# New merge orders for the four engines in the mixer stage of a hybrid recurrent trunk

## The chip, the cores and the metric

The kernel is one program on one core of a Trainium2 chip. The metric is device time in microseconds (us) of one execution, as the median of three runs. The engines named below are PE (TensorE, the matrix engine), DVE (VectorE), ACT (ScalarE), POOL (GpSimd) and SP (SyncE, which here issues DMAs). Each has its own instruction queue and works through it in order; a semaphore wait on one instruction holds everything behind it on that engine.

## The reference

Two layers of a decoder trunk run on 320 tokens: 256 of one prompt and 8 new tokens of each of 8 sequences, model width 1024. Each layer does

```python
h = rmsnorm(x, W['norm_mix'][i])
cp = h @ W['w_in'][i]
ya, sh, Sa = rwkv7_mixer(ca, s_shift[i], s_rwkv[i], ...)    # RWKV-7 time mixing, 6 heads
yb, Sb = retention_mixer(cb, s_ret[i], pos0, ...)           # retention, 4 heads
yc, cv, hc = mamba2_mixer(cc, s_conv[i], s_ssm[i], ...)     # Mamba-2 SSD, 6 heads
x = x + jnp.concatenate([ya, yb, yc], axis=-1) @ W['w_out'][i]
h = rmsnorm(x, W['norm_ffn'][i])
x = x + swiglu(...)   # layer 0;   layer 1: top 2 of 8 experts, moe_swiglu(...)
```

and returns the outputs and every group's recurrent state, for the prompt and for the 8 sequences. All of it is in float32.

## The kernel before, in words

Activations stay on the chip, transposed (features on the partitions, 320 tokens along a row). Weights stream from HBM in slots of 128x1024 floats (SP's queue, a ring of 11). Each slot is split in two parts: ACT copies it to `whi` (line 1472), DVE subtracts to get `wlo` (line 1981), and PE makes each product in three passes (lines 619 to 621).

A layer has four stages: input norm and input projection with the mixers, output projection, feed-forward norm, feed-forward or experts. Only the second half of the first stage is touched here. In it the 28 remaining slots of the input projection run merged with the three mixers. Every mixer is cut into short pieces, and each engine has its own list of which piece comes next. In the lists:

- `in` is a piece of the input projection. On PE it is half a slot (12 products). On ACT the pieces of one slot are the split of a later slot (line 1472) and the copy of the result out of PSUM; on DVE they are the split of a later slot (line 1981) and, for the RWKV columns, the token shift (lines 2093 to 2095), which reads the PSUM bank and so frees it.
- `prep` is the RWKV preparation (decays, keys, bonus), `inv0` to `inv2` the triangular inversions of the three token blocks (prompt 0 to 127, prompt 128 to 255, samples), `cb`, `tok`, `rw` the RWKV chunk products, transposes and recurrence; `sS`, `nS`, `xs`, `xv` the RWKV sample states.
- `rot` and `rt0` to `rt2` are the retention, `conv`, `dt` and `mb0` to `mb2` the Mamba-2 group, `shift` an output DMA, `out` the start of the output projection (on ACT and DVE: the splits of its first two slots).

The helper `weave` walks a list and takes from the named part its code up to the next `yield`. The lists are the strings `PE_TURNS` (181 pieces), `ACT_TURNS` (136), `DVE_TURNS` (226) and `POOL_TURNS` (29), and the same lists serve both layers. Within a part the order is fixed; only how the parts interleave is chosen by the lists. The waits in the code of each piece are on constants and don't depend on the lists.

Some pieces matter later. `inv` on PE: line 785 forms the matrices and waits for DVE's last `prep` products (lines 2146, 2151); line 795 transposes what DVE wrote at line 2220; lines 802, 809, 813 are the levels of the inversion. `rw` on PE: line 881 multiplies the `Rs` that DVE copied (line 2262), ACT copies the result to `SA` (line 1663), line 613 (`mx`) accumulates; after the last chunk ACT copies the outputs to `kp` (line 1667), and lines 908, 912 and 918 are the group norm. `mb` on DVE: line 2427 scales the sample states. ACT's functions lie in table sets, and where the next function is of another set than the last, an ACT_TABLE_LOAD stands in front of it.

After the lists, PE multiplies the 8 slots of the output projection.

Of the kernel before, what the change touches and what calls it, by code (L numbers as in the profile page):

```python
# [143 lines left out]
for _n, _w in [("g_mix", 8), ("g_ffn", 8), ("g_fin", 8), ("mu", A_TILES), ("w0", 3), ("a0", 3), ("k_k", 3),  # L144
# [39 lines left out]
ACT_TURNS = """
    dt in in in in prep prep in in in in prep prep in in prep in in prep in in prep prep in in in in in in in in
    in in in in prep conv in in prep conv prep in in conv in in sS dt dt tok2 conv tok2 dt in in in in conv tok2
    in conv in conv in rw2 in in in in in rw2 rw2 in in mb0 mb0 tok0 in in tok0 mb0 in in rt0 in mb0 mb0 tok0 in
    mb1 rw0 mb1 in mb0 rw2 mb1 rt0 rt0 rw0 mb1 rw0 rw0 mb1 rw0 mb1 tok1 mb2 tok1 tok1 mb2 rt0 rw0 mb2 rw1 rt0
    mb2 rt1 rt1 rt1 rw1 rt1 mb2 mb2 rt1 out out rw1 rw1 rw1 rt2 rw1 rt2 rt2 rt2 rt2
"""  # L190
DVE_TURNS = """
    prep in in in in in in in prep in in in in in in prep in in in prep in prep prep in prep prep in inv2 inv1 in
    inv0 inv1 in inv1 inv0 inv2 inv0 inv2 in inv2 in prep inv0 inv1 inv2 in inv2 inv0 inv1 conv conv conv conv inv1
    in conv conv inv0 inv2 conv conv inv1 inv0 inv2 in conv inv0 conv conv conv cb2 cb2 inv1 inv0 inv0 inv0 in inv1
    conv conv dt conv conv inv0 dt inv1 dt dt dt dt dt dt inv0 inv1 dt dt dt inv0 dt dt in conv conv conv conv in
    conv conv conv conv in conv conv inv1 conv conv rw2 in xs inv1 inv1 in xs nS nS rot xs nS cb0 nS rw2 in nS nS
    rw2 in cb0 cb0 mb0 in rot rot mb0 rt0 rt0 in in in in rw2 mb0 rw2 mb0 rw2 mb0 mb0 mb0 mb0 mb0 mb0 rw0 mb1 rw0
    mb0 rw2 mb1 rw0 mb1 mb1 mb1 mb1 mb1 mb1 rw0 cb1 cb1 cb1 mb1 mb1 rw0 mb1 mb2 rw0 rt0 rw0 rw0 rt0 rw0 rw1 mb2 rt0
    rt0 mb2 mb2 rt0 rw1 rt1 rt1 mb2 mb2 mb2 rw1 rt1 rt1 mb2 mb2 rt1 rt1 rw1 mb2 rt1 out out rt2 rt2 rw1 rw1 rw1 rw1
    rw1 rt2 rt2 rt2 rt2 rt2 rt2  # L200
"""
# [2873 lines left out]
```

## Time and profile before

| | us |
|---|---|
| median of 3 runs (1288.71 to 1290.39) | 1289.28 |
| the profiled execution's own time | 1288.66 |
| its span | 1286.8 |
| PE busy | 1229.0 (96%) |
| DVE busy | 920.9 (72%) |
| ACT busy | 716.3 (56%) |
| POOL busy | 131.5 (10%) |
| merged stage of layer 0 | about 25 to 262 |
| merged stage of layer 1 | about 542 to 781 |

All stretches are in us from the start of the span. The two merged stages are 476 of the 1286.8 us. "PE busy" includes time in which a product runs at half the clock, so the granted clock has to be read beside it.

### The profile page before, as it was taken

The numbers are of one execution on the slowest core, as the hardware profiler recorded it, in microseconds if no ns is written. First come the engines' busy times: TensorE is split into PE (matmuls) and PEld (weight loads), VectorE is DVE, ScalarE is ACT, GpSimd is POOL, SyncE is SP. The second block draws the span as 40 slices with busy tenths as digits, with TensorE's granted clock in tenths as the row PEclk, the third lists the DMA queues.
The fourth block names the chain that finished last, engine by engine and source line by source line (L and its number), as shares of the span: only waits on it lengthen the run. The fifth ranks groups of instructions, "written<-read, shape, count | busy, mean of one in ns | idle before, by whom it ended". The sixth has DMA issues, their size and how long they took to land.

```text
span 1286.8 us, 27073 instructions
## 1 busy us (share of the span) xinstructions
PE 1229.0 (96%) x10557; PEld 1098.7 (85%) x10557; DVE 920.9 (72%) x1477; ACT 716.3 (56%) x1109; POOL 131.5 (10%) x161
## 2 busy tenths in 40 slices
PE   7989999899999999998999989899999999999996
PEld 6979888789999999997988878887888788788785
DVE  7576755666555557857675565588989989998996
ACT  6633345234433334472434534577877878777784
POOL 1021310210000000102121012001010110101010
PEclk9999999789999999999999988999999999999998
DMA  8321331155445443242133106389979979997992
GB/s 295 120 85 46 111 106 35 73 198 188 150 152 168 152 147 132 75 134 70 54 119 107 35 23 232 122 292 330 341 256 356 323 263 344 324 354 253 358 323 104
DMA packets 63835, 236.35 MB, mean 184 GB/s; under 512 B 7536, under 2 KB 7760, under 8 KB 63088
## 3 DMA queue, kind: packets, MB, share of 16 engines
q1 hardware_dynamic: 60960, 221.51, 49.1%
q0 software_dynamic: 2336, 12.81, 2.7%
q8 instruction: 77, 1.26, 0.4%
q10 hardware_dynamic: 432, 0.52, 0.1%
q14 instruction: 30, 0.25, 0.1%
HBM read 225.41 MB, written 8.09 MB: 181 GB/s over the span
## 4 chain that ended last, share of the span: by engine, by line
PE 82%; DVE 10%; ACT 4%; issue 4%; DMA 0%; DVEq 0%; ACTq 0%
PE bank L619 12%; PE bank L621 11%; PE bank L620 11%; PE bank L1409 8%; PE bank L1386 6%; PE bank L1388 6%; PE bank L1387 6%; PE bank L613 3%; PE bank L1306 2%; DVE wlo L1981 2%; ACT whi L1472 2%; PE bank L813 1%; PE bank L802 1%; PE bank L809 1%; PE bank L1351 1%
## 5 line engine op out<-in xcount | busy, mean ns | idle before, releaser
L1472 ACT ACTIVATE whi<-wraw 128x1024 fp32r<-128x1024 f32 x407 | 428.8, 1059 | 354.7 <-PE bank L621 292.5
L1981 DVE TENSOR_TENSOR wlo<-wraw,whi 128x1024 fp32r<-128x1024 f32 x407 | 501.4, 1245 | 170.4 <-ACT whi L1472 162.9
L619 PE MATMUL bank<-hh,whi 128*128 128x320 f32 x576 | 189.1, 328 | 12.6 <-DVE Dx L2095 6.4
L621 PE MATMUL bank<-hh,wlo 128*128 128x320 f32 x576 | 180.5, 313 | 0.0
L620 PE MATMUL bank<-hl,whi 128*128 128x320 f32 x576 | 180.5, 313 | 0.0
L1386 PE MATMUL bank<-whi,hh 128*128 128x512 f32 (+1 forms) x384 | 147.4, 384 | 3.4 <-DVE wlo L1981 2.9
L1388 PE MATMUL bank<-wlo,hh 128*128 128x512 f32 (+1 forms) x384 | 143.5, 374 | 0.0
L1387 PE MATMUL bank<-whi,hl 128*128 128x512 f32 (+1 forms) x384 | 143.3, 373 | 0.0
L619 PEld LDWEIGHTS bank<-hh,whi 128*128 128x128 f32 x576 | 110.3, 191 | 23.9 <-issue 7.9
L619 PE MATMUL bank<-rawh,whi 128*128 128x320 f32 x384 | 119.8, 312 | 0.5 <-DVE rawl L2538 0.3
L621 PE MATMUL bank<-rawh,wlo 128*128 128x320 f32 x384 | 118.9, 310 | 0.0
L620 PE MATMUL bank<-rawl,whi 128*128 128x320 f32 x384 | 118.9, 310 | 0.0
L620 PEld LDWEIGHTS bank<-hl,whi 128*128 128x128 f32 x576 | 110.7, 192 | 0.0
L621 PEld LDWEIGHTS bank<-hh,wlo 128*128 128x128 f32 x576 | 110.5, 192 | 0.0
L1386 PEld LDWEIGHTS bank<-whi,hh 128*128 128x128 f32 x384 | 72.2, 188 | 22.0 <-DVE wlo L1981 6.5
L1388 PEld LDWEIGHTS bank<-wlo,hh 128*128 128x128 f32 x384 | 72.3, 188 | 13.3
L1387 PEld LDWEIGHTS bank<-whi,hl 128*128 128x128 f32 x384 | 72.4, 189 | 10.2
L619 PEld LDWEIGHTS bank<-rawh,whi 128*128 128x128 f32 x384 | 72.6, 189 | 1.1 <-DVE rawl L2538 0.6
L620 PEld LDWEIGHTS bank<-rawl,whi 128*128 128x128 f32 x384 | 72.6, 189 | 0.1
L621 PEld LDWEIGHTS bank<-rawh,wlo 128*128 128x128 f32 x384 | 72.5, 189 | 0.0
L2939 POOL TENSOR_TENSOR x<-x,yt 128x320 f32<-128x320 f32 x28 | 27.2, 992 | 393.3 <-ACT yt L1884 392.9
L619 PE MATMUL bank<-hidh,whi 128*128 128x320 f32 x184 | 56.9, 309 | 1.6 <-DVE hidl L2538 1.0
(427 smaller groups left out, 2084.4 us busy)
## 6 DMA issues: line engine op xcount, KB each, us to landing
wraw<-in_w SPq DMA_DIRECT2D x410, 512.0 KB, 5.0
smb<-in_s_ssm POOLq DMA_DIRECT2D x2, 1536.0 KB, 8.0
out_o_ssm<-smb POOLq DMA_DIRECT2D x2, 1536.0 KB, 7.2
cst<-in_consts SPq DMA_DIRECT2D x1, 2097.0 KB, 13.3
srw<-in_s_rwkv POOLq DMA_DIRECT2D x2, 768.0 KB, 5.9
out_o_rwkv<-srw POOLq DMA_DIRECT2D x2, 768.0 KB, 3.7
x<-in_x SPq DMA_DIRECT2D x2, 640.0 KB, 4.9
cBs<-cB SPq DMA_DIRECT2D x16, 80.0 KB, 2.1
```

Of the source, the lines that this page charges most:

```text
L613: return pe.matmul(out, lhsT, rhs, start=start, stop=stop, skip_group_check=True)
L619: mm(out, hi, rh, start=first, stop=False)
L620: mm(out, hi, rl, start=False, stop=False)
L621: return mm(out, lo, rh, start=False, stop=last)
L1306: m = mm(B[bk][:, (k % 2) * 2 * P:(k % 2 + 1) * 2 * P], htk[z][:, q, k * P:(k + 1) * P], pick[:, q, :, :], start=(q == 0), stop=(q == 2))
L1386: mm(out, hh[:, k, ours], whi[:, r % HI, cols], start=(k == 0), stop=False)
L1387: mm(out, hl[:, k, ours], whi[:, r % HI, cols], start=False, stop=False)
L1388: m = mm(out, hh[:, k, ours], wlo[:, POS[r], cols], start=False, stop=(k == KT - 1))
L1409: m = mm(B[4 + z][:, :], h_[:, f, 0:P], w_[:, z * 512:(z + 1) * 512], start=(f == 0 and q == 0), stop=(f == FT - 1 and q == 2))
L1472: af(whi[:, ring % HI, :], wraw[:, POS[ring], :], ACT.Copy).then_inc(S("slot_hi"), 1)
L1981: tt(wlo[:, POS[ring], :], wraw[:, POS[ring], :], whi[:, ring % HI, :].bitcast(F32), ALU.subtract).then_inc(S("slot_split"), 1)
L2939: tt(x[:, m_, :], x[:, m_, :], yt[:, m_ // 2, :], ALU.add).then_inc(S("yt_free"), 1)
```

## The change

Only the four lists change. Each part's pieces are the same in number and in inner order. On DVE three `in` pieces that hold no instruction come last in the list instead of in the middle. No tile, no buffer, no wait and no operation of the program is edited. Two lines of PE's list stand for the kind of edit:

```diff
-    in in in in in in in in prep in in in in in in in prep in in in prep in in in in in inv2 inv1 inv0 in inv1 inv2
-    inv0 in inv2 in prep inv2 inv0 inv1 in in inv1 inv0 inv2 prep inv1 in inv0 inv2 in inv1 inv0 cb2 cb2 sS sS sS
+    in in in in in in in in prep in in in in in in in prep in in in prep in in in in in in inv2 inv1 inv0 in in inv2
+    inv1 inv0 prep inv2 inv1 in in inv2 inv0 inv2 inv1 inv0 inv1 inv0 prep in in inv0 inv1 in sS inv0 inv2 sS inv0
```

What it does to the instructions at three places, in layer 0 (layer 1 has the same lists):

DVE, end of the RWKV preparation, before. Lines 2144, 2146 and 2151 are the last preparation products, 1981 is a weight split, 2093 to 2095 the token shift of a projection result:

```order
L2144 TENSOR_TENSOR aa<-X_84,aa 128x960
L1981 TENSOR_TENSOR wlo<-wraw,whi 128x1024
L2146 TENSOR_TENSOR aa<-aa,Pi 128x960
L2151 TENSOR_TENSOR Pi<-kp,Pi 128x960
L2093 SCALAR_TENSOR_TENSOR Dx<-bank,par,Dx 128x255
L2094 SCALAR_TENSOR_TENSOR Dx<-bank,par,Dx 128x8x7
L2095 SCALAR_TENSOR_TENSOR Dx<-sh_in,par,Dx 128x8
L2217 TENSOR_TENSOR A<-bank,cst 128x192
```

DVE, the same place, now:

```order
L2144 TENSOR_TENSOR aa<-X_84,aa 128x960
L1981 TENSOR_TENSOR wlo<-wraw,whi 128x1024
L2093 SCALAR_TENSOR_TENSOR Dx<-bank,par,Dx 128x255
L2094 SCALAR_TENSOR_TENSOR Dx<-bank,par,Dx 128x8x7
L2095 SCALAR_TENSOR_TENSOR Dx<-sh_in,par,Dx 128x8
L2146 TENSOR_TENSOR aa<-aa,Pi 128x960
L2151 TENSOR_TENSOR Pi<-kp,Pi 128x960
L1981 TENSOR_TENSOR wlo<-wraw,whi 128x1024
L2217 TENSOR_TENSOR A<-bank,cst 128x192
```

The token shift now stands ahead of the last two preparation products. On PE the matching change is one more half slot ahead of the first inversion product, and two half slots instead of one between the first and the second.

ACT, end of the merged stage, before. Here `s_rr` and `ysq` are norms of the retention and of Mamba, `SA` and `kp` belong to the last RWKV block, `hh` is an operand of the output projection, and the two `whi` rows are the splits of the first two slots of the output projection:

```order
L1663 ACTIVATE SA<-bank 128x192 [waits rw_SA]
L1699 ACTIVATE s_rr<-bank,cst 128x4 [waits rt_ms]
L1730 ACTIVATE ysq<-bank,cst 128x64 [waits mb_ms]
L1734 ACTIVATE hh<-cZ 128x3x64 [waits slot_used,mb_y3]
L1704 ACTIVATE hh<-cB 128x2x128 [waits slot_used,rt_y]
L1472 ACTIVATE whi<-wraw 128x1024 [waits slot_used,slot_in0]
L1472 ACTIVATE whi<-wraw 128x1024 [waits slot_used,slot_in1]
L1667 ACTIVATE kp<-bank 128x3x128 [waits rw_y]
L1670 ACTIVATE Pi<-bank 128x3x128 [waits rw_yd]
```

ACT, the same place, now:

```order
L1699 ACT_TABLE_LOAD
L1699 ACTIVATE s_rr<-bank,cst 128x4 [waits rt_ms]
L1730 ACTIVATE ysq<-bank,cst 128x64 [waits mb_ms]
L1663 ACTIVATE SA<-bank 128x192 [waits rw_SA]
L1667 ACTIVATE kp<-bank 128x3x128 [waits rw_y]
L1734 ACTIVATE hh<-cZ 128x3x64 [waits slot_used,mb_y3]
L1670 ACTIVATE Pi<-bank 128x3x128 [waits rw_yd]
```

One `whi` split went about 20 rows ahead, the other behind the retention's last norm; `kp` follows `SA` directly, and `SA` itself stands behind two norms.

ACT, middle of the merged stage, now. `xs` is the convolution's activation, `stage` a copy of a projection result, `d_wk` an exponential of the Mamba decays:

```order
L1646 ACTIVATE tok<-bank 128x192 [waits rw_tr]
L1472 ACTIVATE whi<-wraw 128x1024 [waits slot_used,slot_in10]
L1568 ACT_TABLE_LOAD
L1568 ACTIVATE xs<-cvx 128x256 [waits cv_done]
L1569 ACTIVATE xs<-cvx 128x64
L1558 ACTIVATE stage<-cv_in 128x8x3 [waits cv_kept,cv_done,slot_used]
L1559 ACTIVATE stage<-bank 128x8x8
L1560 ACTIVATE stage<-bank 128x256
L1634 ACT_TABLE_LOAD
L1634 ACTIVATE d_wk<-bank 128x18 [waits dt_cum]
L1663 ACTIVATE SA<-bank 128x192 [waits rw_SA]
L1568 ACT_TABLE_LOAD
```

The third convolution's activation stood ahead of the sample-state copies and all exponentials of the decays before; now it comes after a weight split that needs a later slot. In one layer's lists there are 22 table loads in all, and there were 19.

## Rows read from the trace of the kernel before

**Rows 1.** The page: busy us, share of the span, instructions.

```profile
PE 1229.0 (96%) x10557; PEld 1098.7 (85%) x10557; DVE 920.9 (72%) x1477; ACT 716.3 (56%) x1109; POOL 131.5 (10%) x161
```

**Rows 2.** Busy time by stretch: length, PE, PEld, DVE, ACT, POOL, clock, DMA.

```profile
25.00:262.00 237.00, 223.16 (x3044) 200.07 (x3042) 151.69 (x332) 108.16 (x216) 43.78 (x47) 0.96 0.26 86
262.00:540.00 278.00, 276.00 (x1873) 273.61 (x1874) 170.92 (x246) 112.44 (x157) 3.72 (x6) 0.99 0.46 152
542.00:781.00 239.00, 225.26 (x3046) 202.02 (x3045) 152.27 (x334) 108.45 (x217) 44.81 (x53) 0.95 0.26 86
```

**Rows 3.** Waits of PE, 25 to 255: who, for whom, sum, times, longest.

```profile
PE bank L619 <- DVE Dx L2095: 3.2, 2, 3.1
PE bank L881 <- DVE Rs L2262: 2.2, 2, 1.5
PE bank L619 <- ACT cZ L1548: 1.4, 1, 1.4
PE bank L908 <- ACT kp L1667: 1.3, 1, 1.3
PE bank L813 <- DVE Wm L2230: 1.1, 1, 1.1
PE bank L795 <- DVE Wm L2220: 1.0, 1, 1.0
...
PE bank L837 <- DVE srw_p L2271: 0.6, 1, 0.6
```

**Rows 4.** Timeline of DVE, end of preparation: start, us, what.

```profile
66.45 1.60 DVE L1981 TENSOR_TENSOR wlo<-wraw,whi 128x1024 fp32r<-128x1024 f32 x1
67.97 1.27 DVE L2146 TENSOR_TENSOR aa<-aa,Pi 128x960 f32<-128x960 f32 x1
69.27 1.52 DVE L2151 TENSOR_TENSOR Pi<-kp,Pi 128x960 f32<-128x960 f32 x1
70.72 0.47 DVE L2093 SCALAR_TENSOR_TENSOR Dx<-bank,par,Dx 128x255 f32<-128x255 f32 x1
71.29 0.34 DVE L2095 SCALAR_TENSOR_TENSOR Dx<-sh_in,par,Dx 128x8 f32<-128x8 f32 x1
```

**Rows 5.** Timeline of PE, four waits, idle time before in brackets.

```profile
71.69 0.41 PE L619 MATMUL bank<-hh,whi 128*128 128x320 f32 x1 [3.06 <-DVE Dx L2095]
...
176.86 0.41 PE L619 MATMUL bank<-hh,whi 128*128 128x320 f32 x1 [1.42 <-ACT cZ L1548]
...
237.66 0.91 PE L881 MATMUL bank<-Rs,TT 64*64 64x64 f32 x12 [1.50 <-DVE Rs L2262]
...
246.29 0.91 PE L908 MATMUL bank<-kp,cst 128*128 128x384 f32 x2 [1.29 <-ACT kp L1667]
```

**Rows 6.** Timeline of DVE: a split in the middle, state scaling near the end.

```profile
145.09 3.70 DVE L1981 TENSOR_TENSOR wlo<-wraw,whi 128x1024 fp32r<-128x1024 f32 x1 [1.72 <-ACT whi L1472]
...
233.53 3.69 DVE L2427 TENSOR_TENSOR smb<-smb,ecb 128x512 f32<-128x512 f32 x6
```

**Rows 7.** Timeline of ACT near the end of the stage.

```profile
222.36 1.28 ACT L1699 ACT_TABLE_LOAD   x1
223.66 0.26 ACT L1699 ACTIVATE s_rr<-bank,cst 128x4 f32<-128x4 f32 x1
...
243.88 1.99 ACT L1472 ACTIVATE whi<-wraw 128x1024 fp32r<-128x1024 f32 x2
245.77 0.47 ACT L1667 ACTIVATE kp<-bank 128x384 f32<-128x384 f32 x1
```

**Rows 8.** Stretches around the clock's falls, columns as in rows 2.

```profile
200.00:237.60 37.60, 33.14 (x690) 28.97 (x688) 25.62 (x70) 16.51 (x34) 1.14 (x2) 1.00 0.06 17
237.60:244.50 6.90, 6.84 (x80) 6.27 (x82) 3.68 (x15) 2.22 (x6) 1.66 (x3) 0.51 0.15 52
247.90:264.90 17.00, 16.74 (x142) 14.01 (x143) 8.31 (x20) 3.69 (x9) 9.31 (x8) 0.50 0.44 156
587.00:592.00 5.00, 3.20 (x14) 2.87 (x14) 1.74 (x4) 0.37 (x2) 1.98 (x3) 0.72 0.24 94
```

More of the change, by code:

```diff
@@ L175 @@
 PE_TURNS = """
-    in in in in in in in in prep in in in in in in in prep in in in prep in in in in in inv2 inv1 inv0 in inv1 inv2
-    inv0 in inv2 in prep inv2 inv0 inv1 in in inv1 inv0 inv2 prep inv1 in inv0 inv2 in inv1 inv0 cb2 cb2 sS sS sS
-    inv0 in inv0 in inv0 inv1 sS inv0 dt tok2 inv1 inv0 tok2 inv1 in inv0 dt in in in tok2 in in inv1 rw2 in in rw2
-    inv1 in in inv1 nS in cb0 nS rw2 in nS rw2 in rw2 in mb0 cb0 cb0 in tok0 in tok0 mb0 in in rt0 rw2 mb0 rt0 in in
-    mb0 in mb0 tok0 in rw0 mb1 rw0 in in rw0 rw0 mb1 rw0 mb1 rt0 rw0 mb1 rw0 rw0 cb1 rw0 mb1 cb1 cb1 rw0 tok1 mb2
@@ L181 @@
-    tok1 tok1 rw0 rt0 rt0 rw1 mb2 rt0 rw1 mb2 rw1 rw1 rt1 mb2 rt1 rw1 rt1 rt1 rw1 rt1 mb2 rt1 rw1 rw1 rw1 rt2 rw1
-    rt2 rw1 rt2 out out rt2 out rt2 rt2
+    in in in in in in in in prep in in in in in in in prep in in in prep in in in in in in inv2 inv1 inv0 in in inv2
+    inv1 inv0 prep inv2 inv1 in in inv2 inv0 inv2 inv1 inv0 inv1 inv0 prep in in inv0 inv1 in sS inv0 inv2 sS inv0
+    sS inv0 in cb2 sS cb2 inv1 dt tok2 inv0 inv1 tok2 inv0 tok2 in in in in dt rw2 inv1 in rw2 inv1 inv0 in in in in
@@ L183 @@
+    in inv1 nS rw2 cb0 in in nS inv1 rw2 in rw2 nS cb0 in mb0 cb0 in in tok0 tok0 rw2 mb0 in mb0 in rt0 tok0 in rt0
+    in mb0 in mb0 in rw0 mb1 in in rw0 mb1 rw0 rw0 mb1 rw0 rt0 rw0 mb1 rw0 rw0 cb1 cb1 rw0 rt0 mb1 cb1 rt0 rw0 tok1
+    tok1 mb2 tok1 rw0 mb2 rw1 mb2 rt0 rw1 rw1 rt1 mb2 rw1 rt1 rw1 rt1 mb2 rt1 rt1 rw1 rt1 rw1 rw1 rw1 rt2 out rw1
+    rt2 rw1 rt2 out rt2 out rt2 rt2
 """
 ACT_TURNS = """
-    dt in in in in prep prep in in in in prep prep in in prep in in prep in in prep prep in in in in in in in in
@@ L186 @@
[L186 to L189, printed above, removed]
+    in in in in prep in in prep in prep prep in in in prep in in prep in in in prep prep in in in in in in in in dt
@@ L190 @@
+    in in in in in prep in prep conv in in in conv sS dt dt tok2 tok2 in in prep tok2 in conv in dt rw2 conv conv in
+    in in in in in in conv in rw2 in rw2 in mb0 conv in in tok0 mb0 mb0 in in in tok0 mb0 mb0 rt0 tok0 in mb1 mb1
+    rw0 rw2 mb1 in mb0 rw0 rt0 mb1 rt0 rw0 rw0 mb1 rw0 out tok1 rt0 mb1 tok1 mb2 tok1 mb2 mb2 rw1 rw0 rt0 rt1 mb2
+    rt1 rt1 rt1 mb2 rw1 rw1 mb2 rw1 rt1 rw1 rt2 rt2 rw1 rt2 rt2 out rt2
 """
 DVE_TURNS = """
-    prep in in in in in in in prep in in in in in in prep in in in prep in prep prep in prep prep in inv2 inv1 in
@@ L193 @@
[L193 to L197, printed above, removed]
@@ L198 @@
-    mb0 rw2 mb1 rw0 mb1 mb1 mb1 mb1 mb1 mb1 rw0 cb1 cb1 cb1 mb1 mb1 rw0 mb1 mb2 rw0 rt0 rw0 rw0 rt0 rw0 rw1 mb2 rt0
-    rt0 mb2 mb2 rt0 rw1 rt1 rt1 mb2 mb2 mb2 rw1 rt1 rt1 mb2 mb2 rt1 rt1 rw1 mb2 rt1 out out rt2 rt2 rw1 rw1 rw1 rw1
-    rw1 rt2 rt2 rt2 rt2 rt2 rt2
+    prep in in in in in in in in prep in in in in in prep in in in prep in prep prep in in prep prep in inv2 in inv2
+    inv1 inv0 inv2 inv0 prep inv1 in inv0 in inv1 inv0 inv2 inv1 inv1 inv2 conv conv conv in inv2 inv0 conv conv
+    inv1 conv inv0 conv inv2 inv0 conv inv1 in conv inv0 conv conv inv0 in inv1 inv2 inv0 inv0 cb2 conv cb2 conv
@@ new lines @@
+    inv1 conv dt conv inv0 in dt inv1 dt conv dt dt dt dt dt inv0 dt dt dt conv dt conv inv1 rw2 conv conv conv dt
+    conv in in in conv conv conv conv inv0 inv1 xs conv conv inv1 in nS rw2 in nS xs in inv1 xs nS cb0 rot nS nS nS
+    cb0 rw2 mb0 cb0 in rot rot mb0 rt0 mb0 rt0 rw2 rw2 mb0 in mb0 mb0 mb0 mb0 mb0 mb0 in rw2 rw0 mb1 mb1 rw0 mb1 mb1
+    rw0 mb1 mb1 mb1 rw0 mb0 cb1 mb1 rw2 cb1 cb1 mb1 mb1 rw0 mb1 mb2 rw0 rt0 rw0 rt0 rw1 rw0 mb2 mb2 rt0 mb2 rt0 rw1
+    rt1 rt1 mb2 mb2 mb2 rw1 rt1 rt0 rt1 mb2 mb2 rt1 out rw1 rt1 mb2 rw0 rt2 rt2 rw1 rw1 rw1 rw1 rt2 rw1 rt2 rt1 rt2
@@ L201 @@
+    rt2 rt2 out rt2 in in in
 """
 POOL_TURNS = """
-    prep prep shift conv conv prep conv conv conv conv xv conv conv rot xv xv xv xv mb0 rot mb1 mb2 rt1 conv mb1 rt2
-    mb2 mb2 rt2
+    prep prep conv conv conv prep xv conv conv conv xv conv xv rot conv xv rot mb0 xv mb1 mb2 rt2 mb2 shift rt2 rt1
+    conv mb2 mb1
 """
```

## The prediction

> **What bounds the kernel now.** I read the page first, then the busy time by stage, then PE's own waits, and last the timelines around each wait. The page [rows 1] shows PE busy 96% of the span, so only PE's idle time and its time at a low clock can be won by an order. The stretches [rows 2] say where that is: from 262 to 540 PE is busy 276.0 of 278 us, while each merged stage has it idle 13.8 us (237.0 − 223.16; 239.0 − 225.26 = 13.7 in layer 1). DVE is busy 64% and ACT 46% there, so neither is a bound by its sum; what ends PE's waits is one late instruction at a time. The list of PE's waits [rows 3] names them: the six largest and one of 0.6, 10.8 us together; the first is a projection product (L619) that once stands 3.1 us for the token shift L2095. Layer 1 runs the same lists and has the same idle time, so everything below is worked for one layer and doubled.
>
> The clock is the second loss. Near the end of the stage the granted clock is 0.5, which is 1.2 GHz instead of 2.4, for 6.9 and 17.0 us [rows 8], after 37.6 us in which PE was busy 33.14, or 88%.
>
> **The change part by part.** The operations stay, so no busy time of PE, DVE or POOL goes or comes. ACT gets 3 table loads more a layer at 1.28 us each [rows 7], 3.8 us on an engine with 129 us idle in the stage (237.0 − 108.16 [rows 2]). What counts is which wait ends when.
>
> Place A, 66 to 90 us. Before, DVE finishes a split at 68.05, then does the two products L2146 and L2151, and only then the token shift, which ends at 71.63 [rows 4]; PE, waiting since 68.63 (71.69 − 3.06 [rows 5]), goes on at 71.69. Now the shift comes directly after the split. It takes 0.92 us from its first start to its last end, so it ends at 68.97 and PE goes on at about 69.0, 2.7 us earlier. The products it overtook end 0.9 us later, at about 71.7. PE has two half slots before it needs them instead of one; a half slot is 12 products at 0.147 us each (276.0 us for 1873 of them [rows 2]), 1.8 us, so PE comes to the inversions at 72.5 and doesn't wait. At that point it has done 1.8 us more work than before and stands 1.0 us earlier (before: 71.69 + 1.8 = 73.5), together 2.8. Next, the wait of L795 for L2220 (1.0 us) has two half slots over it instead of one and should go; following DVE's new row of work I find two new short waits, 0.1 us at the second inversion group and 0.5 at the third, because the bonus products L2155 now stand ahead of one L2220. Place A: −2.8 − 1.0 + 0.6 = −3.2 us.
>
> Place B, 100 to 150. The wait of L813 for L2230 (1.1 us [rows 3]) came after a split that took 3.70 us [rows 6], where the one in rows 4 took 1.60; while it ran, POOL was in the rotary products of the retention. That POOL piece now stands behind two RWKV state pieces, and no split of DVE starts while it runs. −1.1. Against that, ACT's third convolution activation now waits behind a weight split for a later slot and pays a load of 1.28; DVE's next convolution tap waits for it, and the `Rs` copy and a split stand behind the tap. I follow this to two new waits of PE, 0.5 and 0.8 us: +1.3. The bounds are 0, if the split is ready one slot earlier than I think, and +3.7, if a whole load and a whole activation piece come on top twice over. I take 1.3, as the rows nearest to it (1.0 to 1.4 [rows 3]) are waits of this kind.
>
> Place C, 176.9. L619 waits 1.42 us for ACT's L1548, a table load and a copy behind a split [rows 5]. PE now has about 1.5 us more of other work (a transpose group and a norm product) in front of it. −1.4.
>
> Place D, 205 to 262. Four waits change. L837 (0.6 [rows 3]) goes because DVE updates the RWKV state ahead of the Mamba state. The 1.50 us before L881 at 237.66 comes from the six scalings that hold DVE 3.69 us [rows 6]; they still stand in front, but PE now has two more norm sums and the second half of a chunk to do meanwhile. −1.5. The 1.29 us before L908 goes: ACT did two splits, 1.99 us, just ahead of `kp` [rows 7], and now does none there. −1.3. A new table load stands in front of `s_rr`, 1.28, with some 0.5 us of it uncovered; DVE's `cZ` chain comes 0.6 us later since the sum in front of it waits its turn, and PE's cover for that is a transpose group. Together +0.9. The later `mb` pieces come up to 1 us earlier, which gives the retention's last block the same. −1.0. Place D: −0.6 − 1.5 − 1.3 + 0.9 − 1.0 = −3.5. The bounds are −6.5, all waits shown for this place plus the second half-clock piece shortened, and +1.
>
> Here a rule of the Trainium skill bears on the added loads. The rows have the load at 1.28 us and the function 0.02 us behind its end [rows 7]. The page "ScalarE: Activation LUTs", section "What ACT_TABLE_LOAD costs", adds a drain of about 1.38 us to the 1.28 of every switch, 2.66 in all; by it the three new loads would cost ACT 8.0 us a layer instead of 3.8 and the new waits in places B and D would be some 2.8 us longer, two loads of 1.38 more, which makes 1278 of the forecast (my estimate from that page). The trace shows no such drain, so the sum keeps 1.28.
>
> Past the lists nothing should come late. The second `whi` and `wlo` split for the output projection now stand near the end, but PE first has the rest of one slot, 2.2 us, to do. POOL issues four output DMAs ahead of its last state product, about 2.3 us; PE wants that product 12 us later. If this cover were gone it would cost those 2.3 us a layer.
>
> Sum for a layer: −3.2 − 1.1 + 1.3 − 1.4 − 3.5 = −7.9 us; for two, −15.8. The profiled execution took 1288.66 us (span 1286.8, and 1.9 around it), 0.6 under the median. 1288.66 − 15.8 = 1272.9, so I say 1273.
>
> **The rivals.**
>
> 1. *Given back in the middle.* From 90 to 165 us PE would run about 3 us ahead of its old times, but DVE and ACT have to keep up, with more inversion pieces in a row on PE and fewer projection products over them. The old order had almost no wait from 100 to 145. For it: three of my covers there are under 0.5 us. Against: DVE is only 64% busy. If place A and B come to nothing (−3.2 − 1.1 + 1.3 = −3.0), −4.9 a layer remains, and if half of D goes too, −3.2. Time: about 1281.
>
> 2. *The clock stays up.* If the waits that go in place D keep PE above the share it had before the fall, the 17.0 us at 0.5 [rows 8] shorten. At most 8.5 us of it could go; the hand-overs between ACT, DVE and PE in the last retention block (ACT and DVE pieces of 0.3 to 0.6 us between PE pieces) take back about half. −4.5 a layer more: 1264. For it: PE was only 12% idle ahead of the fall. Against: waits of 0.6 remain in the same stretch, and the pieces there stay small.
>
> 3. *Slower, by the clock in the middle.* Should the new waits in place B be 2 us each and follow closely, PE would be as idle as in layer 1 at 587 to 592, 3.20 of 5 us busy and a clock of 0.72 [rows 8]. Around 120 to 140 us PE does projection products back to back, so a stretch like the one of 17.0 us at half would cost its whole 8.5 us. With 4 − 1.3 = 2.7 us more waiting, −7.9 + 2.7 + 8.5 = +3.3 a layer, 1295. It decides from a stretch of about 10 us at half on (7.9 − 2.7 = 5.2 us lost). For it: the order of ACT there is the one thing that looks worse than before. Against: in layer 0 the 3.1 us wait of place A made no fall.
>
> 4. *The orders change, and nothing comes of it.* The waits move to other instructions and sum to the same 13.8 us, as PE's chains are as long as before. 1288.7. For it: every piece has the same inputs. Against: places A and the `kp` row are plain, a wait that stands behind work that it doesn't need.
>
> **How the numbers follow.** The forecast has a chance of 0.47, rival 1 0.20, rival 2 0.13, rival 3 0.10, rival 4 0.10. The predicted time is 1273. The range of 8 in 10 runs from 1261, under rival 2 with its fullest clock gain, to 1287, over rival 1. No change means within 0.2%, 2.6 us, about what a measurement of this kernel can tell. Faster: 0.47 + 0.20 + 0.13, and a little of rival 4: 0.81. Same: 0.08. Slower: 0.11.
>
> **What would show it.** In the profile after: PE's wait at L619 for L2095 under 0.5 us, and the sum of PE's waits in the merged stage of layer 0 near 6 (13.8 idle before, less 7.9); L813 for L2230, L619 for L1548, L837 for L2271 and L908 for `kp` gone from PE's waits; new waits at L881 or L619 around 125 to 140 us of about 1.3 together; the merged stage ending near 254 instead of 262; two falls of the clock at its end still there. I am wrong if PE's idle time in the stage stays above 11 us a layer, if the granted clock falls in the middle of a merged stage, or if it stays up at the end.

## The result

The changed kernel took 1274.08 us (median of 4 runs, 1271.64 to 1275.14), the kernel before 1289.84 in the same comparison (4 runs, 1288.71 to 1292.28): a ratio of 0.9873, 95% interval 0.9852 to 0.9893. It is faster by 1.3%, and 1273 was forecast. The sections below show that the time came out almost as forecast by luck: two steps of the forecast failed, with errors of opposite sign. Of the 56 executions of the kernel before that were recorded with their clock, one had a mean clock of 0.737 and a span of 1507.3 us; it is left out everywhere.

The page of the profiled execution after (1275.14 us, span 1273.3), the row that answers to [rows 1]:

```profile
PE 1217.8 (96%) x10557; PEld 1092.2 (86%) x10557; DVE 920.4 (72%) x1477; ACT 721.5 (57%) x1115; POOL 132.2 (10%) x161
```

The span is 13.5 us shorter, and PE's busy time, with the same 10557 products, is 11.2 us shorter. So PE's idle time fell by only 2.3 us in the whole kernel, where the forecast wanted 15.8. A busy time that shrinks at an unchanged count of products points at the clock: mean clocks of 0.974 and 0.980 over the two spans are 66.9 and 50.9 us at half clock. The busy time by stretch, columns as in [rows 2]:

```profile
25.00:262.00 237.00, 224.51 (x3074) 203.89 (x3073) 153.62 (x338) 112.10 (x220) 43.79 (x47) 0.96 0.26 88
262.00:540.00 278.00, 275.36 (x1875) 272.36 (x1874) 173.86 (x250) 114.74 (x161) 7.39 (x16) 1.00 0.45 153
542.00:781.00 239.00, 226.53 (x3092) 205.52 (x3091) 154.15 (x335) 114.31 (x222) 45.05 (x49) 0.96 0.28 91
```

From 25 to 262 us PE is idle 12.5 us (13.8 before), although this stretch now holds 6.6 us of the next stage. PE's waits in layer 0, as in [rows 3]:

```profile
PE bank L619 <- DVE Dx L2095: 2.2, 3, 1.2
PE bank L619 <- ACT cZ L1548: 1.5, 1, 1.5
PE bank L1035 <- ACT rsq L1696: 1.2, 1, 1.2
PE bank L1078 <- DVE seg L2378: 1.2, 1, 1.2
PE bank L802 <- DVE TT L2238: 0.9, 1, 0.9
PE bank L809 <- DVE Wm L2230: 0.9, 1, 0.9
PE bank L619 <- DVE wlo L1981: 0.9, 1, 0.9
PE bank L619 <- ACT cB L1544: 0.8, 1, 0.8
...
PE bank L908 <- ACT kp L1667: 0.6, 1, 0.6
...
PE bank L881 <- DVE Rs L2262: 0.5, 1, 0.5
```

The list is longer and its rows are smaller. L813, L795 and L837 are gone as forecast, and L908 is halved. Both old waits of L881 (at 225 and 238 us) are gone; the 0.5 shown is a new one at 138. L619 for `cZ` stayed, and most of the others are new.

To say where time went, both traces need points of equal work. PE's list has 181 pieces (one name of the list each), and at its 49th and 138th piece both orders have done exactly the same pieces. The 49th comes at about 100 us, in the triangular inversions; the 138th is a read product (L837) of RWKV block 1, at about 212. Up to the 49th, to the 138th and to the end of the stage, before:

```profile
25.00:101.20 76.20, 71.43 (x760) 66.19 (x760) 51.90 (x102) 39.89 (x82) 13.82 (x13) 1.00 0.32 108
101.20:211.94 110.74, 107.35 (x1602) 96.38 (x1600) 68.94 (x146) 48.50 (x93) 18.75 (x24) 1.00 0.27 86
211.94:261.12 49.18, 43.50 (x690) 37.38 (x689) 30.56 (x83) 18.89 (x40) 11.21 (x11) 0.80 0.14 52
```

and after:

```profile
25.00:98.70 73.70, 71.41 (x772) 67.18 (x771) 51.92 (x103) 37.92 (x75) 12.21 (x11) 1.00 0.34 113
98.70:213.00 114.30, 108.17 (x1590) 98.74 (x1591) 65.99 (x143) 53.91 (x103) 20.54 (x24) 0.97 0.25 83
213.00:255.40 42.40, 38.34 (x691) 32.13 (x690) 31.21 (x84) 17.95 (x39) 8.24 (x8) 0.90 0.14 52
```

Length less PE's busy time is idle time, and the third number from the right is the mean granted clock. A stretch at half clock is charged here with half its length. The head (first row) is 2.5 us shorter, all of it idle time. The middle is 3.6 us longer: idle time +2.7, 6.9 us at half clock where there was none, +3.4, and 2.6 less for the rest of the work. The tail is 6.8 us shorter: idle time −1.6 (5.7 to 4.1), and the clock 0.80 to 0.90, which is 19.7 us at half clock (2 x 0.20 x 49.18) against 8.5, −5.6. Layer 1 repeats it: its middle is 3.6 longer, its tail 6.7 shorter. Up to the tail the new order has gained nothing. Charged like this, most of what the tail gains is the clock; the runs e9 and the table below show that a microsecond at half clock costs nearer 0.3 than 0.5, which leaves the clock about half of it.

### The profile page after: what moved, and what is told of

Same layout as the page of the kernel before. It is cut to its first block, busy times and chain, and to the rows that moved or that the text cites. A ratio compares the mean times of both kernels' runs of the same rounds, so it can differ in the third digit from the quotient of the medians.

```text
span 1273.3 us, 27099 instructions
## 1 busy us (share of the span) xinstructions
PE 1217.8 (96%) x10557; PEld 1092.2 (86%) x10557; DVE 920.4 (72%) x1477; ACT 721.5 (57%) x1115; POOL 132.2 (10%) x161
## 3 DMA queue, kind: packets, MB, share of 16 engines
q1 hardware_dynamic: 60960, 221.51, 49.3%
q8 instruction: 77, 1.26, 0.4%
## 4 chain that ended last, share of the span: by engine, by line
PE 81%; DVE 8%; ACT 7%; issue 3%; DMA 0%; ACTq 0%; DVEq 0%
PE bank L619 12%; PE bank L621 11%; PE bank L620 11%; PE bank L1409 8%; PE bank L1386 6%; PE bank L1388 6%; PE bank L1387 6%; PE bank L613 4%; DVE wlo L1981 2%; PE bank L1306 2%; ACT whi L1472 2%; PE bank L802 1%; PE bank L1351 1%; PE bank L1335 1%; PE bank L813 1%
## 5 line engine op out<-in xcount | busy, mean ns | idle before, releaser
L619 PE MATMUL bank<-hh,whi 128*128 128x320 f32 x576 | 188.7, 328 | 13.5 <-DVE Dx L2095 4.5
L619 PEld LDWEIGHTS bank<-hh,whi 128*128 128x128 f32 x576 | 111.0, 193 | 22.7 <-issue 7.8
L619 PE MATMUL bank<-rawh,whi 128*128 128x320 f32 x384 | 120.2, 313 | 0.5 <-DVE rawl L2538 0.3
L1387 PEld LDWEIGHTS bank<-whi,hl 128*128 128x128 f32 x384 | 72.4, 189 | 10.2
L619 PEld LDWEIGHTS bank<-rawh,whi 128*128 128x128 f32 x384 | 73.0, 190 | 1.1 <-DVE rawl L2538 0.6
L1409 PE MATMUL bank<-whi,hidh 128*128 128x512 f32 x176 | 57.9, 410 | 0.6 <-DVE wlo L1981 0.6
```

The source lines that it names most:

```text
L619: mm(out, hi, rh, start=first, stop=False)
L1387: mm(out, hl[:, k, ours], whi[:, r % HI, cols], start=False, stop=False)
L1409: m = mm(B[4 + z][:, :], h_[:, f, 0:P], w_[:, z * 512:(z + 1) * 512], start=(f == 0 and q == 0), stop=(f == FT - 1 and q == 2))
```

## The experiments

Each kernel has the operations of the kernel before; where only lists differ, a hybrid follows one order up to a point of equal work and the other behind it, on all four engines. Each was timed in five rounds beside the kernel before.

**Run e1, the new head and middle.**

```diff
 PE_TURNS, pieces 26 to 49 (50 to 138 and the other engines' lists likewise)
-in inv2 inv1 inv0 in inv1 inv2 inv0 in inv2 in prep inv2 inv0 inv1 in in inv1 inv0 inv2 prep inv1 in inv0
+in in inv2 inv1 inv0 in in inv2 inv1 inv0 prep inv2 inv1 in in inv2 inv0 inv2 inv1 inv0 inv1 inv0 prep in
```

> New orders on all four engines up to PE's 138th piece (the first head norm of the Mamba chunks, about 212 us), the old orders behind it. Theory T (all of the gain lies behind that piece, since at it the new kernel stands 1.07 us later than the old in layer 0 and 1.1 us more behind than it began in layer 1): 1288.7 + 2 x 1.1 = about 1291, PE's idle time before 212 us about 8.4 us, the merged stage ending about 263. Rival F (the forecast's places A, B and C are worth -3.2 + 0.2 - 1.4 = -4.4 a layer): 1280. Rival I (the halves only work together): 1289 here and in the run of the other half.

(The 138th piece is not a head norm but the read product L837.) Measured: ratio 0.9989 (0.9973 to 1.0005), 1290.24 us. Theory T holds: the places A, B and C together, costed at −4.4 us a layer, brought nothing. In its trace the head is 2.6 us shorter and the middle 5.0 us longer than before, with 10.2 us at half clock in it.

**Run e2, the new tail.**

```diff
 PE_TURNS, pieces 139 to 162, and 163 to 181
-rw0 mb1 cb1 cb1 rw0 tok1 mb2 tok1 tok1 rw0 rt0 rt0 rw1 mb2 rt0 rw1 mb2 rw1 rw1 rt1 mb2 rt1 rw1 rt1
+cb1 rw0 rt0 mb1 cb1 rt0 rw0 tok1 tok1 mb2 tok1 rw0 mb2 rw1 mb2 rt0 rw1 rw1 rt1 mb2 rw1 rt1 rw1 rt1
-rt1 rw1 rt1 mb2 rt1 rw1 rw1 rw1 rt2 rw1 rt2 rw1 rt2 out out rt2 out rt2 rt2
+mb2 rt1 rt1 rw1 rt1 rw1 rw1 rw1 rt2 out rw1 rt2 rw1 rt2 out rt2 out rt2 rt2
```

> The complement: old orders up to PE's 138th piece, new orders behind it. T: -6.7 us a layer, the merged stage of layer 0 ending near 255, one fall of the clock of 3.4 us and one of 10.2 in it instead of 6.9 and 17.0; 1288.7 - 13.5 = 1275. F: place D alone, -3.5 a layer, 1281.7. I: 1289.

Measured: 0.9881 (0.9857 to 0.9905), 1277.64 us, nearly all of the change's gain. Theory T is nearest (2.6 us off); F is 4 us off and I falls. Its tails of layer 0 and 1:

```profile
213.30:255.90 42.60, 38.28 (x691) 32.63 (x690) 29.47 (x79) 17.93 (x39) 7.25 (x7) 0.92 0.14 50
725.20:769.10 43.90, 39.58 (x689) 33.41 (x688) 30.61 (x82) 17.93 (x39) 7.69 (x7) 0.87 0.15 49
```

**Runs e3 and e11, the head alone, and one step of it.** e3 takes the new orders up to the 49th piece (the diff of e1). e11 moves one piece of DVE's list:

```diff
 DVE_TURNS, end of the preparation
-in prep in prep prep in prep prep in inv2 inv1 in
+in prep in prep prep in in prep prep inv2 inv1 in
```

> New orders only up to PE's 49th piece (about 101 us), old ones behind it. In the two traces the new kernel is 2.5 us ahead at that piece in both layers. T (the lead is real and was lost behind it, to two waits of 0.9 us at 105 to 110 us and 6.8 us at half clock): the old middle waits only 0.15 us from 100 to 145, so the lead stays: 1288.7 - 5 = 1283.7. F: -3.2 a layer, 1282.3. Rival G (DVE and ACT are as late as before whatever PE does, so that any lead is given back by 118 us): 1288.7, with 2 us or more of new waits from 100 to 125.

> The kernel before with one step of DVE moved, and nothing on the other engines: the token shift (L2093 to L2095) ahead of the preparation's products L2146 and L2151. Forecast's place A without its half slots on PE: the wait of 3.06 us at 71.69 falls to 0.4; then the inversion comes 0.9 us later on DVE over one half slot of PE instead of two, at most 0.9 us of new wait: -1.8 to -2.7 a layer, 1285.1 to 1283.3. Rival Q (the swap alone is worth nothing, because the inversion that stood behind the products is then what PE waits for; the 2.85 us of the run e3 came from PE's half slots): 1288 to 1290, with a new wait of 2 us or more at L772 to L802 between 72 and 80 us.

Measured: e3 0.9942 (0.9919 to 0.9965), 1283.98 us, as theory T says, and rival G falls; e11 0.9931 (0.9913 to 0.9949), 1282.92, slightly more gain than its range. The waits of PE in e11 from 25 to 100 us:

```profile
PE bank L795 <- DVE Wm L2220: 1.0, 1, 1.0
PE bank L619 <- DVE Dx L2095: 0.3, 1, 0.3
PE bank L785 <- DVE Pi L2151: 0.2, 1, 0.2
```

The wait of 3.06 us [rows 5] is 0.33, the inversion's cover is short by 0.2 only, and PE stands 2.56 us earlier at the 49th piece, as against 2.66 in e3. So the token shift ahead of two products is nearly the whole of place A; rival Q falls. PE's shifted half slots and the removed wait of L795 are paid back by a new wait at 62.55 us, and the wait for the shift itself is still 0.88. DVE near 70 us, and PE's two waits, in the changed kernel:

```profile
68.24 1.60 DVE L1981 TENSOR_TENSOR wlo<-wraw,whi 128x1024 fp32r<-128x1024 f32 x1
...
70.33 0.34 DVE L2095 SCALAR_TENSOR_TENSOR Dx<-sh_in,par,Dx 128x8 f32<-128x8 f32 x1
70.60 1.15 DVE L2146 TENSOR_TENSOR aa<-aa,Pi 128x960 f32<-128x960 f32 x1
```

```profile
62.55 0.42 PE L619 MATMUL bank<-hh,whi 128*128 128x320 f32 x1 [1.21 <-DVE Dx L2095]
70.73 0.41 PE L619 MATMUL bank<-hh,whi 128*128 128x320 f32 x1 [0.88 <-DVE Dx L2095]
```

The long wait took the clock with it as well. Four traces have DVE's old order here (before, e2, e5, e9), and PE waits 3.1 us for L2095 in each of their eight heads. In seven of these 3.4 to 6.8 us at half clock follow at once; the fall at 589 [rows 8] is one of them. In the ten traces with the shift moved ahead no head of the twenty has a fall, and e11 differs from the kernel before in that one step only. The heads of layer 0 and layer 1, e2 and then e11 (those of layer 1 don't begin at the same piece, so that only their clock compares):

```profile
25.00:102.56 77.56, 72.89 (x760) 67.66 (x760) 51.86 (x102) 39.84 (x82) 13.81 (x13) 0.98 0.33 107
538.27:614.39 76.12, 71.82 (x753) 66.68 (x754) 50.25 (x101) 38.24 (x80) 13.80 (x13) 0.98 0.32 108
```

```profile
25.00:98.64 73.64, 71.86 (x763) 66.71 (x763) 51.30 (x102) 39.73 (x82) 13.91 (x13) 1.00 0.34 113
538.01:613.62 75.61, 73.22 (x769) 67.49 (x769) 53.27 (x106) 41.67 (x85) 16.65 (x23) 1.00 0.33 111
```

**Run e4, head and tail without the middle.** (The diffs of e1 for the pieces 26 to 49 and of e2, with the old pieces 50 to 138.)

> New orders up to PE's 49th piece, old ones from there to the 138th, new ones behind it: the two parts in which the new kernel gains, without the middle in which it loses. T with parts that add: 1275 - 5 = 1270. G: 1275, as with the tail alone. I: 1274 or more, not under the changed kernel.

Measured: 0.9793 (0.9766 to 0.9820), 1266.62 us. That is under the changed kernel, so I and G fall, and it is more than the gains of e2 and e3 together (23.5 us against 12.4 and 6.1); theory T's 1270 is 3.4 too high. Its old middle takes what the old middle took before, with a clock of 1.00:

```profile
98.66:209.20 110.54, 107.14 (x1591) 96.16 (x1592) 68.41 (x145) 50.09 (x98) 20.84 (x25) 1.00 0.27 87
```

What the new middle does wrong is in the changed kernel's timeline, all engines:

```profile
102.59 1.28 ACT L1568 ACT_TABLE_LOAD   x1
...
104.98 0.46 DVE L2108 TENSOR_SCALAR cvx<-stage,par 128x344 f32<-128x344 f32 x1 [7.18 <-ACT stage L1560]
...
105.47 0.35 DVE L2238 TENSOR_TENSOR TM<-TM,bank 128x192 f32<-128x192 f32 x1
...
106.24 0.92 PE L802 MATMUL bank<-TM,A 64*64 64x64 f32 x24 [0.93 <-DVE TT L2238]
...
109.30 0.89 PE L809 MATMUL bank<-Wm,TT 64*64 64x32 f32 x24 [0.91 <-DVE Wm L2230]
```

DVE stands idle for 7.18 us at a convolution tap that needs ACT's copy `stage`. ACT had itself waited 9.16 us for PE, until 100.53, to get a buffer for a split; then it does the split, a copy, the table load and an activation, and only then `stage`. In e4, which stands within 0.02 us of this kernel at the 49th piece, the load ran at 98.06, ahead of the split, and the tap began at 103.99, 1.0 us earlier. Behind the tap stands L2238, for which PE waits. The granted clock then falls:

```profile
110.28:117.10 6.82, 6.82 (x88) 6.70 (x85) 1.97 (x7) 0.00 (x0) 0.00 (x0) 0.51 0.01 2
```

This is half clock, 1.2 GHz, for 6.8 us, in both layers at the same place, the 3.4 us of the account above. All six new middles on record (the changed kernel, e1, e7) have such a stretch, of 6.8 to 10.2 us, and none of the sixteen old ones has.

**Run e6, less of the old middle.** (New again from the 87th piece.)

> New orders up to PE's 49th piece, old from there to the 86th (about 144 us), new ones behind it. Theory M (the new middle loses only from the 49th to the 86th piece, where its two waits of 0.9 us and 6.8 us at half clock are; from the 86th to the 138th the new kernel is 1.84 us faster than the old in both layers): 1266.6 - 3.7 = 1263. Rival N (those 1.84 us are only PE catching up on engines that had waited for it): 1266 to 1268.

Measured: 0.9807 (0.9778 to 0.9835), 1265.89 us, the same as e4. The middle took 110.07 us against 110.54; rival N holds, theory M falls. So what the new middle loses lies between the 49th and the 86th piece.

**Runs e9 and e10, the tail cut at the 162nd piece.** (The second pair of lines in the diff of e2: alone in e9; e10 is e6 with the first pair old again.)

> Old orders up to PE's 162nd piece (about 234 us), new ones for the last 19 of each layer. In the traces these 19 take 27.3 us in the old order (233.81 to 261.12) and 19.1 in the new (236.34 to 255.41), while the pieces from the 138th to the 162nd take 1.5 us more in the new. Theory L (the last 19 pieces hold all of the gain, by their own order): 1288.7 - 2 x 8.2 = 1272, under the run e2. Rival K (they are only quick because the new pieces ahead of them had fed ACT and DVE earlier, 1.5 us well spent): 1278 or more, above the run e2.

> The kernel of the run e6 with the old orders also from PE's 138th to its 162nd piece: new up to the 49th, old to the 86th, new to the 138th, old to the 162nd, new for the last 19. Theory L: 1.5 us a layer less than e6, 1265.9 - 3 = 1263. Rival K: 1266 to 1272, slower than e6.

Measured: e9 0.9909 (0.9886 to 0.9932), 1280.65 us; e10 0.9861 (0.9836 to 0.9885), 1273.35. Both are slower than theory L said and go rival K's way, e10 by 1.4 us more than it allowed: the pieces 139 to 162 belong to the gain. The trace of e9 shows more than it was made for. Its tails of layer 0 and layer 1, the same instructions in the same order:

```profile
214.33:264.06 49.73, 47.22 (x691) 40.37 (x690) 31.19 (x82) 18.49 (x39) 7.70 (x7) 0.70 0.12 44
733.93:776.30 42.37, 37.66 (x691) 31.98 (x690) 30.61 (x81) 18.42 (x39) 7.71 (x7) 0.93 0.15 52
```

Layer 0 has less idle time (2.5 against 4.7 us) and is 7.4 us longer, at a clock of 0.70 instead of 0.93. In one execution, at an equal order, the clock made a difference as large as the whole gain of a tail. It also gives a price: 29.8 us at half clock against 5.9, so 23.9 us more of it cost 7.4, or 0.31 us each, and not 0.5, since PE's waits shrink while its products take longer.

**Run e5, PE kept busy in the old tail.**

```diff
+            def keep_busy(out, n):
+                for _ in range(n):
+                    mm(out[:, 0:P], C("cmat"), C("ident"), start=True, stop=True)
...
+                    if (b, c) == (1, 1):
+                        keep_busy(B[3], 6)
                     pe.wait_ge(S("rw_Rc"), cb + c + 1)
...
+                if b == 1:
+                    keep_busy(B[2], 5)
                 pe.wait_ge(S("rw_yc"), it)
```

> The kernel before with its old orders, and products added that nobody reads: six products of 128 columns on PE just ahead of its wait for the second chunk of the last RWKV block (L881, 1.50 us of waiting at 237.66) and five ahead of its wait for kp (L908, 1.29 us at 246.29), about 0.22 us each by L997's rows, 1.3 and 1.1 us. Every other wait and every order is the old one. Theory C (the clock falls because PE stood idle, and most of the tail's gain is the clock): the 19.7 us at half clock per layer behind PE's 138th piece shrink to 10 or less, so 5 us or more a layer come back: 1279 or below, although no wait for another engine has gone. Rival W (the gain is the waits alone, and the clock falls through the narrow products that run there, 64 columns wide): 1289 to 1291, half-clock time unchanged.

Measured: 0.9983 (0.9954 to 1.0012), 1288.43 us. The median is rival W's, less 0.6 us. The profiled execution had 12.4 us at half clock in layer 0's tail and 20.0 in layer 1's. The filling worked at one of the two waits only: the 1.50 us ahead of L881 is gone, but the wait for `kp` is now 1.60 us behind the added products, and in layer 0 one of 2.12 for `rsq` comes later, with which the clock falls (line numbers behind the added lines are up by 9):

```profile
245.06 1.38 PE L853 MATMUL bank<-cst 128*128 128x128 f32 x10
248.04 0.91 PE L917 MATMUL bank<-kp,cst 128*128 128x384 f32 x2 [1.60 <-ACT kp L1676]
...
257.60 0.59 PE L1044 MATMUL bank<-cst,rsq 128*64 128x4 f32 x4 [2.12 <-ACT rsq L1705]
```

The 12 runs fall into two groups: six of 1283.5 to 1286.5 us with a mean clock of 0.983 or 0.984, a clock that no run of the kernel before had, and six of 1290.4 to 1296.9 us with 0.968 to 0.975. The mean clock is 0.978 against 0.972 for the kernel before in that comparison. So the added products do bring clock back, in half of the executions, and their own 3.0 us of PE's time a layer use it up: at an equal clock e5 is 2.5 us longer than the kernel before (table below). Theory C is supported by this, not shown: the waits were only in part filled, and no trace is from the faster group.

**Run e7, ACT's splits ahead of `kp` again.**

```diff
 ACT_TURNS
-mb1 rw0 out tok1 ... mb2 rw1 rw1 mb2 rw1 ... rt2 rt2 out rt2
+mb1 rw0 tok1 ... mb2 rw1 out out rw1 mb2 rw1 ... rt2 rt2 rt2
```

> The changed kernel with one thing undone: ACT's two weight splits for the output projection stand directly ahead of kp again. Forecast's term alone (the wait for kp is longer by 1.3 us a layer, the clock as it is): 1274 + 2.6 = 1276.7. Theory C (a longer wait there also makes the half-clock stretch that follows 3.4 us longer or more): 1274 + 2 x (1.3 + 1.7) = 1280. Rival W0 (PE's path at the end goes by the retention, and kp is covered): 1274.

Measured: 0.9869 (0.9839 to 0.9900), 1273.70 us, no change against the changed kernel. In its timeline ACT does both splits in a gap in which it had to wait for PE anyway (2.44 us in the changed kernel), and PE's wait is the 0.6 of the list above:

```profile
239.82 2.01 ACT L1472 ACTIVATE whi<-wraw 128x1024 fp32r<-128x1024 f32 x2
242.38 0.49 ACT L1667 ACTIVATE kp<-bank 128x384 f32<-128x384 f32 x1 [0.55 <-PE bank L613]
```

The forecast's reason for the term of `kp`, that it stood behind two splits [rows 7], is half of it. In the kernel before, the splits stood just behind two operand copies that wait for DVE:

```profile
243.55 0.42 ACT L1704 ACTIVATE hh<-cB 128x256 fp32r<-128x256 f32 x1 [0.61 <-DVE cB L2355]
```

So they began at 243.88 and ran past 245.00, when PE was done with what `kp` copies; `kp` began at 245.77, and that is the 0.7 us by which the wait shrank. The other 0.6 is the copy itself and is in every trace. In e7 the copies stand behind `kp`, and the splits are done in time.

**Runs e8 and e12, the last norm of the retention.** e8 changes PE's list of e4, e12 changes three lists of e6:

```diff
 PE_TURNS, the last five (e8 and e12)
-out rt2 out rt2 rt2
+out out rt2 rt2 rt2
 DVE_TURNS (e12)
-rw1 rw1 rw1 rw1 rt2 rw1 rt2
+rw1 rw1 rw1 rt2 rw1 rw1 rt2
 ACT_TURNS (e12)
-rt2 rt2 rw1 rt2 rt2 out rt2
+rt2 rt2 rt2 rw1 rt2 out rt2
```

> The kernel of the run e4 with one more step of order on PE: the third product group of the output projection ahead of the retention's last norm sum (L1035) instead of behind it, 1.06 us of work into a wait of 1.47 us. Theory: its operands are there (it never waited), so 1.06 us a layer go, 1264.5; by theory C the 6.8 us at half clock behind that wait shorten by 3.4 as well, 1.7 us more a layer: 1261. Rival: its operands come only after the norm sum, 1266.6 or slower.

> The kernel of the run e6 with three steps of order at the end of the merged stage: DVE adds the retention's last output (L2329, 0.27 us) ahead of the RWKV product L2293 (1.28 us) instead of behind it, ACT squares it (L1696) ahead of the RWKV copy L1679, and PE has the third product group of the output projection ahead of the norm sum L1035. In e6 that sum waits 1.5 us for the square. Theory D (the wait is made by what stands ahead on DVE and ACT, so that moving PE's group alone, in e8, only moved it): the wait goes, 0.4 to 0.6 us come back ahead of L1041, -1.0 us a layer: 1265.9 - 2 = 1264, with PE's idle time behind its 138th piece at 3.3 instead of 4.3 us. Rival E (the path at the end goes by the products and the sample states, which come no earlier): 1266, idle time 4 or more.

Measured: e8 0.9801 (0.9773 to 0.9828), 1265.78 us; e12 0.9782 (0.9764 to 0.9800), 1261.87, the fastest median here. In e8 the moved products ran ahead of L1035 without a wait, but its wait fell only from 1.47 to 1.03 us, and a new one of 0.55 stands ahead of L1041. So neither theory (1264.5) nor rival (1266.6 or slower) is confirmed; 0.8 us under e4, in another comparison, is no difference. The wait in e6, and the same place in e12:

```profile
246.24 0.40 PE L1035 MATMUL bank<-cst,rsq 128*64 128x4 f32 x4 [1.47 <-ACT rsq L1696]
```

```profile
248.31 0.40 PE L1035 MATMUL bank<-cst,rsq 128*64 128x4 f32 x4
...
249.97 0.45 PE L1041 MATMUL bank<-cst,s_rr 64*64 64x64 f32 x8 [1.26 <-DVE s_rr L2344]
```

The wait for the square is gone, as theory D has it, but the next one, for `s_rr`, took 1.26 us of it back: the path goes PE, ACT, DVE, PE, and PE has nothing left to put over it. Idle time in the tail is 4.2 us against 4.3, so theory D's 3.3 is wrong and rival E right on idle time. The median is 4.0 us lower than e6's all the same, with a mean clock of 0.989 against 0.986; e12 and e6 were not run side by side and their intervals overlap, so this last step isn't settled. That e4, e6, e8 and e12 beat both kernels is: their intervals lie below that of the changed kernel.

**All runs together.** Every run has a span and a mean granted clock, so orders and clock can be told apart without a profile. Within one kernel the span falls by 0.74 us for every 0.001 of clock (fitted within 14 kernels, 140 runs). As 0.001 of 1290 us is 2.6 us at half clock, this is 0.29 us for each of them, the price that e9's two tails gave. Taking every kernel's mean to a clock of 1 by that slope:

| kernel | runs | mean span | mean clock | span at clock 1 |
|---|---|---|---|---|
| before | 55 | 1289.3 | 0.972 | 1268.1 |
| after | 4 | 1271.9 | 0.982 | 1258.1 |
| e1 head and middle | 12 | 1288.7 | 0.969 | 1265.7 |
| e2 tail | 6 | 1275.4 | 0.982 | 1261.8 |
| e3 head | 7 | 1282.5 | 0.972 | 1261.5 |
| e4 head and tail | 5 | 1264.2 | 0.988 | 1255.0 |
| e5 filled waits | 12 | 1287.0 | 0.978 | 1270.6 |
| e6 less of the old middle | 6 | 1264.2 | 0.986 | 1254.0 |
| e11 one step | 6 | 1281.2 | 0.975 | 1262.6 |
| e12 norm first | 5 | 1261.2 | 0.989 | 1253.1 |

Of the 17.4 us between the means of before and after, 10.0 remain at equal clock and 7.4 are the clock's. For the tail alone (e2) it is 6.3 and 7.6 of 13.9; for the one step of the head (e11) 5.5 and 2.6 of 8.1. The middle takes clock away: e1 has the head's gain and yet the lowest clock of all. The traces agree on the tail. The eight old ones (before, e1, e3, e11) take 49.3 us on average with 19.7 at half clock, the ten new ones (after, e2, e4, e6, e7) 41.9 with 6.2; at 0.3 us each the clock is 4.1 of these 7.4, and the order 3.3.

## Why the number was right and the reasons half wrong

- **Place A, −3.2 a layer.** Right in mechanism, and a little large. −2.5 in the trace, −2.56 with the DVE step alone. Of the rest, L795's 1.0 us did go, but the new wait of 1.21 us at 62.55 was not seen, and the wait for the shift is 0.88 instead of under 0.5. What the step gives beside it, the half-clock stretch behind the old wait, up to 1.7 us in layer 1, was put at nothing, although its fall at 589 stood in [rows 8].
- **Place B, +0.2.** What was named came as named. L813's 1.1 us went, and where the third convolution's activation runs behind a split and a table load (133.86 to 135.14), two new waits stand, 0.46 and 0.89 us, forecast as 0.5 and 0.8:

```profile
137.89 0.56 PE L881 MATMUL bank<-Rs,TT 64*64 64x64 f32 x12 [0.46 <-DVE Rs L2262]
...
143.38 0.39 PE L619 MATMUL bank<-hh,whi 128*128 128x320 f32 x1 [0.89 <-DVE wlo L1981]
```

  The step that failed is what the forecast left out: the same mechanism at the first table load of this stretch, at 102.59, which put 0.93 and 0.91 us of waits at 105 to 110 and the half-clock stretch behind them. These were put at nothing. The runs e4 and e6 show that the loss lies there, between the 49th and the 86th piece; that it is this load and split which make it is read from the timeline, and no run moves them alone. The load itself was 1.28 us as in [rows 7] and the next function started 0.01 us later (102.59 + 1.28, then L1568 at 103.88), so the drain that the Trainium skill's page "ScalarE: Activation LUTs" ("What ACT_TABLE_LOAD costs") adds does not explain these waits.
- **Place C, −1.4.** Failed. The wait for `cZ` is 1.46 us, at 185, where it was 1.42. It is the length of one chain, from PE's last product on a buffer over ACT's split and load to the copy, and PE has 1.6 us of work beside that chain in either order, not 1.5 more. Two more waits came, 0.79 for `cB` at 171 and 0.64 at 176.
- **B and C together.** The middle costs +3.6 instead of saving 1.2, or +4.2 without L837's 0.6, which did go and was counted under place D.
- **Rival 3, a fall of the clock in the middle**, happened, on a smaller scale: 6.8 us at half, up to 3.4 lost, where it had 17 us and decided from 10. Because it was a rival and not a term, the sum lacked it.
- **Place D, −3.5.** The sign is right, the size half of it. The tail brought −6.8, beyond the bound of −6.5. By waits it was −1.6: both waits of L881 went and `kp` shrank, but by 0.7 and not 1.3 (e7), and the new waits for `seg` (1.2), `rsq` (1.2), `s_rr` (0.5) and `SA` (0.4) were costed at 0.9 together. The rest goes with the half-clock stretches, 19.7 us to 8.5, worth 3.4 to 5.6 us, which the forecast held fixed and gave only to rival 2, and there as "stays up". The two falls at the stage's end are still there as forecast, at 3.4 and 10.2 us instead of 6.9 and 17.0.
- **The sum.** −3.2, −1.2 and −3.5 were forecast, −2.5, +3.6 and −6.8 came in layer 0. The errors of +0.7, +4.8 and −3.3 leave −5.7 instead of −7.9. The other −7.8 are −3.4 up to layer 1's 49th piece, where the fall at 589 is gone, +3.6 and −6.7 in its middle and tail, and −1.3 behind them. A fall of 3.4 us at 821 is gone too, but that is chance: e5, e6, e8, e11 and e12 have one there. That all this adds up to −13.5 where −15.8 was forecast is luck. The conditions under which I had called myself wrong, over 11 us idle in the stage and a fall of the clock in its middle, are both met.

What stays open is what in the new tail keeps the clock up. Idle time isn't enough of an answer: e9's two tails contradict it, and e5's added products kept the clock up in half of its executions only. The Trainium skill's page "TensorE: Matmul & The Clock Gate", section "A second HAM failure mode: psum-queue depth-cycling", tells of a bf16 kernel with products of 512 columns in which frequent micro-idles between groups of products make the clock swing. The many short waits of these tails may be of that kind, yet no run here separates short waits from one long one.

## What to carry to other kernels

Compare two orders at points of equal work, and split each stretch into idle time, half-clock time and the rest, before you credit a wait; a busy time that falls at a constant count of products hints at the clock. Take the price of half-clock time from executions of one order, as waits shrink beside it. Cut a reordering at such points and run the parts: here one part of three lost what another won, and leaving it out gave −2.1% instead of −1.3%. Cost a table load or a split by what stands behind it on the next engine and on the one after that, and write a possible clock fall into the sum as a term with a chance, not beside it.

## What the runs showed of the hardware

- Executions of one kernel differ in their mean granted clock, 0.962 to 0.978 over 55 runs of the kernel before, and their spans follow it (1284.3 to 1295.5 us). Most of the spread of a kernel's times is this (correlation −0.96).
- A microsecond at half clock costs this kernel about 0.3 us: 7.4 us for 23.9 in e9's two tails, 0.29 by the slope within 14 kernels.
- A wait of PE of 3.1 us was followed by 3.4 to 6.8 us at half clock in seven of eight places (before, e2, e5, e9); with the wait at 0.3 us (e11) or at 1.2 and 0.9 (e3) there was none.
- The half-clock stretches in the tails changed from layer to layer and from kernel to kernel at an equal order: old tails had 11.4 to 27.7 us (before, e1, e3, e11), the new ones 1.6 to 11.4 (after, e2, e4, e6 to e8, e12). Only as sets of several tails do two orders compare.
- A half slot of twelve projection products takes 1.76 us behind another one and mostly 1.96 behind small products. The new middle enters such a run 16 times and the old 19 times; that is 0.6 us.
- ACT's table load took 1.28 us each time, and the next function began 0.01 to 0.02 us behind it.
